# Differential attention in an encoder block: the weighted sum of a tile moved one step later on TensorE

## The chip, the cores and the metric

The kernel runs on one core of one Trainium2 chip. The metric is the device time of one execution in microseconds. The engines are called PE (TensorE: matrix products and transposes; PEld is its weight load), DVE (VectorE), ACT (ScalarE), POOL (GpSimd) and SP (SyncE, which issues DMAs). Each engine runs its own list of instructions in order, and the lists are tied together by semaphores alone: every wait and every count is written by hand.

## The reference, cut to what matters

One encoder layer over a prompt of 1024 tokens and a sample of 512, each with 16 learned meta tokens in front: a norm, one projection, eight heads of neighbourhood attention and four heads of differential attention, an output projection, and a mixture of 16 experts. The change lies in the differential heads:

```python
def _diff_attention(q, k, v, lam, lambda_init, subln):
    def attend(qb):
        s = jnp.einsum('bqhcd,bkhcd->bhcqk', qb, k).astype(jnp.float32) * scale
        p = jax.nn.softmax(s, axis=-1)
        a = (p[:, :, 0] - lam * p[:, :, 1]).astype(v.dtype)
        return jnp.einsum('bhqk,bkhe->bqhe', a, v)
...
    o = _rmsnorm(o, subln, SUBLN_EPS) * (1.0 - lambda_init)
```

Each head has two score maps (c = 0 and 1), each with its own softmax; their weighted difference multiplies the values.

## The kernel before, in words

A unit is one differential head; there are four, and the last (unit 3, `last` in the code) is treated apart. A unit has DS = 14 tiles of queries: two tails of 32 rows (meta tokens), then four tiles of the sample (512 keys each) and eight of the prompt (1024 keys each); in unit 3 the prompt's tiles come first. The loop over s goes through all of them as a software pipeline on PE, DVE and ACT, and in units 0 to 2 the projection for the next unit's queries, keys and values (`project`, 12 chunks, each in two halves of 12 products) is woven into the steps 0 to 11. Steps 12 to 14 have no projection.

What a tile n passes through:
- `scores` (L1706, PE): two products by key block, one for each map c, into PSUM banks 0 to 3.
- Evacuation of scores (L1285, DVE): out of PSUM into `e_df`, with the row's minimum for the softmax (`nmax`), for c = 0 and then 1.
- `scores_exp` (L889, ACT): the exponentials, with the sums (`ssum`).
- Combine (L1255 to L1260, DVE): the two maps become one.
- Turning (L1749 and L1751, PE): transposes of the combined weights into banks 4, 5 and, for the meta tokens, 6.
- `weights_to_rows` (L746 by way of `copy`, ACT) for bank 4, and copies by DVE (L1296, L1298) for banks 5 and 6, into `et_df`.
- Weighted sum (L1767 and L1769, PE): `et_df` times the values `v`, into bank 6 in units 0 to 2 and bank 7 in unit 3.
- `mix` (L1273, DVE): the sum, scaled, out of PSUM; SP stores it (L687).
- Squares of it (L880, ACT) for the norm.

The values of the next unit are turned by `v_rows` (L1586, L1588, PE) in steps 9 to 12, into bank 5, and copied out by `evac_v` (L1102, L1104, DVE). In units 0 and 1 (and once more in unit 0) `split_wq` splits the weights of a coming projection into a high part on ACT and a low part on DVE (L1091), in steps 5, 9 and 13. `rotate` (DVE) applies the rotary embedding to the next unit's queries and keys in steps 2 to 9; before it SP's `swap_halves` (L608) exchanges halves, once the rotation of the chunk before is done. In unit 3 `split_wo` does the same split for the output projection's weights.

At a unit's start PE makes products of 16 columns, the scores against the meta tokens (L1719, 52 of them); DVE turns these into `nsm` and `nmm`, for which `scores(0)` waits (`df_msn`).

The order on each engine in step s of units 0 to 2, before the change:
- PE: scores of s; projection half 0; turning of s-1; projection half 1; weighted sum of s-1; `v_rows`.
- DVE: `evac_v`; combine of s-1; `mix` of s-2; evacuation of scores of s; copies of s-1; splits; `rotate`.
- ACT: evacuation of the projection; splits; squares of s-3; copy of s-1; exponentials of s.

In unit 3 PE does scores of s, turning of s-1 and the weighted sum of s-2; DVE does combine of s-1, `mix` of s-3, evacuation of s, copies of s-1; ACT has the exponentials ahead of its copy. There the weighted sum of n waits for `mix` of n-1, since bank 7 is single:

```python
                        if last:
                            pe.wait_ge(df_mix, u * DS + n + CREDIT)
```

In units 0 to 2 it is turning that waits for `mix`, as the meta tokens' transpose shares bank 6 with the sum.

Of the kernel before, what the change touches and what calls it, by code (L numbers as in the profile page):

```python
# [26 lines left out]
ALU = mybir.AluOpType  # L27
# [3 lines left out]
P = 128  # L31
# [15 lines left out]
UNITS = 4  # L47
# [87 lines left out]
def build(nc, x_all, w_in, w_out, w_router, w_gate, w_up, w_down, rpb, meta_bias, lambdas, vecs,  # L135
# [12 lines left out]
    with ctx:  # L148
# [593 lines left out]
        def _(act):  # L742
# [120 lines left out]
            for u in range(UNITS):  # L863
                last = u == UNITS - 1
                for s in range(DS + 3 + last):
# [16 lines left out]
                    def scores_exp():  # L882
# [9 lines left out]

                    def weights_to_rows():
# [12 lines left out]
                    if not last and s < DS:  # L906
                        scores_exp()
# [131 lines left out]
        def _(dve):  # L1039
# [191 lines left out]
            for u in range(UNITS):  # L1231
# [14 lines left out]
                for s in range(DS + 3 + last):  # L1246
                    if not last and 0 <= s - 10 < 4:
                        evac_v(UNITS + u + 1, s - 10)
                    if 0 <= s - 1 < DS:
# [12 lines left out]
                                                 op0=ALU.mult, op1=ALU.add).then_inc(df_c, 1)  # L1262
                    n = s - 2 - last
# [12 lines left out]
                    if s < DS:  # L1276
                        t, rows, keep, k0, kt = DFS[u][s]
                        w = kt * P + N_META
                        if s >= 2:
                            dve.wait_ge(df_e, 2 * (u * DS + s - 1))  # L1280
                        dve.tensor_copy(e_df[0:rows, s % 2, :, kt * P:w], nsm[0:rows, :, t * N_META:(t + 1) * N_META])
                        for c in range(2):
                            dve.wait_ge(df_s, 2 * (u * DS + s) + c + 1)

                            dve.tensor_scalar(e_df[0:rows, s % 2, c, 0:kt * P],  # L1285
                                              ps[0:rows, 2 * c * BANK:2 * c * BANK + kt * P], -1.0,
                                              nmm[0:rows, c, t:t + 1], ALU.mult, ALU.min,
                                              accum_out=nmax[0:rows, s % 2, c:c + 1]).then_inc(df_m, 1)
# [258 lines left out]
        def _(pe):  # L1547
# [143 lines left out]
            for u in range(UNITS):  # L1691
# [17 lines left out]

                pe.wait_ge(qk_rot, ROPES * (u + 1))  # L1710
# [13 lines left out]
                v = vs[u % 2]  # L1724
# [6 lines left out]
                for s in range(1, DS + 1 + last):  # L1731
                    if s < DS:
                        scores(s)
                    if not last and s < NCH:
                        project(UNITS + u + 1, s, 0, 7, 1)
                    if s - 1 < DS:
                        n = s - 1
                        t, rows, keep, k0, kt = DFS[u][n]
                        b = n % 2
                        pe.wait_ge(v_evac, 4 * (u + UNITS + 1) + (0 if last else min(max(s - 9, 0), 4)) + CREDIT)  # L1740
                        pe.wait_ge(df_c, u * DS + n + 1)
                        pe.wait_ge(df_et_a, u * DS + n)
                        pe.wait_ge(df_et_d, u * DS + n + CREDIT)
                        if not last or n == 0:
                            pe.wait_ge(df_mix, u * DS + n + CREDIT)
                        if rows < P:
                            apart(pe)
                        for j in range(kt):
                            pe.transpose(ps[:, 4 * BANK + j * P:4 * BANK + j * P + rows],  # L1749
                                         e_df[0:rows, b, 0, j * P:(j + 1) * P], ident[0:rows, 0:rows])  # L1750
                        pe.transpose(ps[0:N_META, 6 * BANK:6 * BANK + rows],  # L1751
                                     e_df[0:rows, b, 0, kt * P:kt * P + N_META], ident[0:rows, 0:rows]).then_inc(df_t, 1)
                    if not last and s < NCH:
                        project(UNITS + u + 1, s, 1, 7, 1)
                    n = s - 1 - last
                    if 0 <= n < DS:
                        t, rows, keep, k0, kt = DFS[u][n]
                        b = n % 2
                        pe.wait_ge(df_et_a, u * DS + n + 1)
                        pe.wait_ge(df_et_d, u * DS + n + 1 + CREDIT)  # L1760
                        if last:
                            pe.wait_ge(df_mix, u * DS + n + CREDIT)
                        if rows < P:
                            apart(pe)
                        bank = 6 + last
                        o = ps[0:rows, bank * BANK + OCOL:bank * BANK + OCOL + P]
# [303 lines left out]
```

## Time and profile before

| | us |
|---|---|
| median of 3 runs | 3156.03 |
| lowest and highest run | 3152.79, 3158.81 |
| profiled execution, its own time | 3157.51 |
| span of the profiled execution, first to last instruction | 3155.7 |
| PE busy | 2971.7 (94%) |
| DVE busy | 1874.3 (59%) |
| ACT busy | 1478.7 (47%) |
| POOL busy | 174.9 (6%) |

The profiled execution lies 1.5 us above the median; the instructions span 1.8 us less than its time. Busy times of engines overlap, so they don't add up to the span. The four differential units run from 502.3 us (first 16-column products of unit 0) to about 999 us; before them lie the norm, the first projection and the neighbourhood heads, after them the output projection, the routing and the experts.

### The profile page before, as it was taken

The numbers are of one execution on the slowest core, as the hardware profiler recorded it, in microseconds if no ns is written. First come the engines' busy times: TensorE is split into PE (matmuls) and PEld (weight loads), VectorE is DVE, ScalarE is ACT, GpSimd is POOL, SyncE is SP. The second block draws the span as 40 slices with busy tenths as digits, with TensorE's granted clock in tenths as the row PEclk, the third lists the DMA queues.
The fourth block names the chain that finished last, engine by engine and source line by source line (L and its number), as shares of the span: only waits on it lengthen the run. The fifth ranks groups of instructions, "written<-read, shape, count | busy, mean of one in ns | idle before, by whom it ended". The sixth has DMA issues, their size and how long they took to land.

```text
span 3155.7 us, 49922 instructions
## 1 busy us (share of the span) xinstructions
PE 2971.7 (94%) x19549; PEld 2785.3 (88%) x19549; DVE 1874.3 (59%) x2998; ACT 1478.7 (47%) x2506; POOL 174.9 (6%) x179
## 2 busy tenths in 40 slices
PE   7999999999988993999999999999999999999993
PEld 6888888777855883999999999999999999999992
DVE  6223335755666346766766766766766666676672
ACT  4223322433334222655655655655555555565562
POOL 1000000000001000010011011010011011001001
PEclk9999999999989995999999999999999999999996
DMA  5322221110011434777877877778777777777774
GB/s 153 99 73 67 70 64 37 32 29 26 26 61 57 134 127 134 221 236 228 245 226 228 247 221 234 240 224 237 235 228 237 231 231 236 228 231 237 226 223 177
DMA packets 637872, 528.25 MB, mean 167 GB/s; under 512 B 30757, under 2 KB 618663, under 8 KB 637651
## 3 DMA queue, kind: packets, MB, share of 16 engines
q1 hardware_dynamic: 629458, 499.46, 51.1%
q0 software_dynamic: 8192, 25.70, 4.1%
q8 instruction: 156, 2.56, 0.3%
q14 instruction: 66, 0.53, 0.1%
HBM read 472.36 MB, written 40.79 MB: 163 GB/s over the span
## 4 chain that ended last, share of the span: by engine, by line
PE 75%; DVE 5%; DMA 2%; issue 1%; ACT 1%; POOL 0%; SPq 0%; DVEq 0%; POOLq 0%; ACTq 0%
PE ps L1889 39%; PE ps L1890 18%; PE ps L1574 5%; PE ps L1799 4%; PE ps L1769 2%; PE ps L1706 2%; DVE e_df L1285 1%; PE ps L1934 1%; PE ps L1749 1%; PE ps L1821 1%; PE ps L1883 1%; DMA y_dram<-yo 1%; PE ps L1767 1%; PE ps L1719 0%; DVE top_v L1370 0%
## 5 line engine op out<-in xcount | busy, mean ns | idle before, releaser
L1889 PE MATMUL ps<-xe,w_hi 128*128 128x392 f32 x4096 | 1195.6, 364 | 1.6 <-DVE xe L1480 1.6
L1890 PE MATMUL ps<-xe,w_lo 128*128 128x196 f32 x4096 | 1034.2, 252 | 0.0
L1467 DVE TENSOR_TENSOR w_lo<-raw,w_hi 128x2048 fp32r<-128x2048 f32 x384 | 875.5, 2284 | 0.2 <-issue 0.2
L1890 PEld LDWEIGHTS ps<-xe,w_lo 128*128 128x128 f32 x4096 | 784.1, 191 | 0.0
L1889 PEld LDWEIGHTS ps<-xe,w_hi 128*128 128x128 f32 x4096 | 770.2, 188 | 1.9 <-DVE xe L1480 1.9
L746 ACT ACTIVATE w_hi<-raw 128x2048 fp32r<-128x2048 f32 x384 | 731.8, 1910 | 11.8 <-DMA raw<-w_down_dram 11.8
L1889 PE MATMUL ps<-hid,w_hi 128*128 128x392 f32 x2048 | 609.4, 366 | 0.0
L1890 PE MATMUL ps<-hid,w_lo 128*128 128x196 f32 x2048 | 516.8, 252 | 0.0
L1890 PEld LDWEIGHTS ps<-hid,w_lo 128*128 128x128 f32 x2048 | 391.4, 191 | 0.0
L1889 PEld LDWEIGHTS ps<-hid,w_hi 128*128 128x128 f32 x2048 | 384.5, 188 | 0.0
L1500 DVE TENSOR_TENSOR gusum<-ps,part 128x392 f32<-128x392 f32 x256 | 145.0, 566 | 395.7 <-ACT part L746 395.7
L746 ACT ACTIVATE part<-ps 128x392 f32<-128x392 f32 x256 | 127.4, 498 | 511.5 <-PE ps L1890 511.5
L1574 PE MATMUL ps<-hT_hi,wq_hi 128*128 128x384 f32 (+1 forms) x768 | 284.8, 371 | 4.9 <-DVE hT_lo L1084 4.1
L1574 PE MATMUL ps<-hT_lo,wq_hi 128*128 128x384 f32 (+1 forms) x768 | 266.0, 346 | 0.0
L1574 PE MATMUL ps<-hT_hi,wq_lo 128*128 128x384 f32 (+1 forms) x768 | 265.7, 346 | 0.0
L1574 PEld LDWEIGHTS ps<-hT_hi,wq_hi 128*128 128x128 f32 x768 | 148.2, 193 | 36.9 <-issue 27.8
L1521 DVE TENSOR_TENSOR yT<-ps,y_part 128x196 f32<-128x196 f32 x128 | 46.2, 361 | 198.2 <-ACT y_part L746 196.4
L746 ACT ACTIVATE y_part<-ps 128x196 f32<-128x196 f32 x128 | 42.3, 330 | 249.2 <-PE ps L1890 249.2
L1574 PEld LDWEIGHTS ps<-hT_lo,wq_hi 128*128 128x128 f32 x768 | 148.6, 193 | 0.3
L1574 PEld LDWEIGHTS ps<-hT_hi,wq_lo 128*128 128x128 f32 x768 | 147.9, 193 | 0.4
L889 ACT ACTIVATE e_df<-e_df,nmax 128x1040 f32<-128x1040 f32 (+3 forms) x112 | 111.7, 1000 | 66.4 <-DVE e_df L1285 66.4
L2005 POOL DMA_INDIRECT residual_rows<-ye,idx_scatter x32 | 49.5, 1546 | 1619.8 <-DVE ye L1488 1614.9
(182 smaller groups left out, 3223.2 us busy)
## 6 DMA issues: line engine op xcount, KB each, us to landing
raw<-w_gate_dram SPq DMA_DIRECT2D x128, 1024.0 KB, 5.2
raw<-w_up_dram SPq DMA_DIRECT2D x128, 1024.0 KB, 5.2
raw<-w_down_dram SPq DMA_DIRECT2D x128, 1024.0 KB, 5.3
wqkv<-w_in_dram SPq DMA_DIRECT2D x24, 512.0 KB, 4.0
xt<-x_all_dram SPq DMA_DIRECT2D x12, 512.0 KB, 4.7
v_na<-v SPq DMA_DIRECT2D x64, 96.0 KB, 2.3
mixed_heads<-mix SPq DMA_DIRECT2D x96, 64.0 KB
mixs<-mixed_heads SPq DMA_DIRECT2D x12, 512.0 KB, 4.0
```

The lines of the kernel that those rows point to most:

```text
L746: return act.activation(out, in_, ACT.Copy, scale=scale)
L889: act.activation(e_df[0:rows, s % 2, c, 0:w], e_df[0:rows, s % 2, c, 0:w], ACT.Exp, bias=nmax[0:rows, s % 2, c:c + 1], scale=-1.0, accum_o ...
L1467: dve.tensor_tensor(w_lo[:, n % NW, :], raw[:, n % NRAW, :], w_hi[:, n % NW, :].bitcast(f32), ALU.subtract).then_inc(lo_done, 1)
L1500: dve.tensor_tensor(gusum[:, m % 2, :, :], src[:, :, 0:SLOTS], part[:, m % 2, :, :], ALU.add).then_inc(sum_done, 1)
L1521: dve.tensor_tensor(yT[:, d, :], ps[:, off:off + SLOTS], y_part[:, d % 2, :], ALU.add).then_inc(yT_done, 1)
L1574: ins = pe.matmul(ps[:, off:off + c1 - c0], wt[:, p, k, :], x[:, k, c0:c1], start=(k == 0 and j == 0), stop=(k == KD - 1 and j == 2))
L1706: ins = pe.matmul(ps[0:rows, o + j * 512:o + (j + 1) * 512], q, kT[f, (k0 + 4 * j) * P:(k0 + 4 * j + 4) * P], start=True, stop=True)
L1769: ins = pe.matmul(o, et_df[:, b, j * P:j * P + rows], v[:, k0 + j, :], start=False, stop=(j == kt - 1))
L1799: ins = pe.matmul(ps[0:rows, off:off + 512], x[:, b, k, 0:rows], w[:, k, n * 512:(n + 1) * 512], start=(k == 0 and j == 0), stop=(k == KD ...
L1889: pe.matmul(out, w_hi[:, slot, cols], x.rearrange("p h n -> p (h n)"), start=first, stop=False)
L1890: return pe.matmul(out[:, 0:SLOTS], w_lo[:, slot, cols], x[:, 0, :], start=False, stop=last)
L2005: pool.indirect_dma_start(out=acc_d, out_offset=bass.IndirectOffsetOnAxis(ap=idx_scatter[:, hh:hh + 1], axis=0), in_=ye[:, hh, :], in_offs ...
```

## The change: what it does

On PE, in units 0 to 2, the weighted sum of tile s-2 now stands in step s, between the scores of s and the projection half; `v_rows` follows it; then come the projection half, the turning of s-1 and the other half. The weighted sum of a unit's last tile moves into the next unit, behind its 16-column products. Turning waits for `mix` only ahead of its last transpose. On DVE the evacuation of scores comes ahead of `mix`, and `evac_v` behind it; this block of DVE's loop has no case apart for unit 3. On ACT the exponentials come ahead of the copy in all units, as they did in unit 3. PE's order in unit 3 stays.

```diff
@@ ACT
-                    if last and s < DS:
-                        scores_exp()
-                    if 0 <= s - 1 < DS:
-                        weights_to_rows()
-                    if not last and s < DS:
-                        scores_exp()
...
@@ DVE
                 for s in range(DS + 3 + last):
-                    if not last and 0 <= s - 10 < 4:
-                        evac_v(UNITS + u + 1, s - 10)
                     if 0 <= s - 1 < DS:
                         n = s - 1
...
+                    if s < DS:
+                        t, rows, keep, k0, kt = DFS[u][s]
+                        w = kt * P + N_META
+                        if s >= 2:
+                            dve.wait_ge(df_e, 2 * (u * DS + s - 1))
+                        dve.tensor_copy(e_df[0:rows, s % 2, :, kt * P:w], nsm[0:rows, :, t * N_META:(t + 1) * N_META])
+                        for c in range(2):
+                            dve.wait_ge(df_s, 2 * (u * DS + s) + c + 1)
+
+                            dve.tensor_scalar(e_df[0:rows, s % 2, c, 0:kt * P],
...
                     n = s - 2 - last
                     if 0 <= n < DS:
...
+                    if not last and 0 <= s - 9 < 4:
+                        evac_v(UNITS + u + 1, s - 9)
                     if 0 <= s - 1 < DS:
...
@@ PE
+                def turned_weights(n):
+                    t, rows, keep, k0, kt = DFS[u][n]
+                    b = n % 2
+                    s = n + 1
+                    pe.wait_ge(v_evac, 4 * (u + UNITS + 1) + (0 if last else min(max(s - 8, 0), 4)) + CREDIT)
+                    pe.wait_ge(df_c, u * DS + n + 1)
+                    pe.wait_ge(df_et_a, u * DS + n)
+                    pe.wait_ge(df_et_d, u * DS + n + CREDIT)
+                    if last and n == 0:
+                        pe.wait_ge(df_mix, u * DS + CREDIT)
...
+                    for j in range(kt):
+                        pe.transpose(ps[:, 4 * BANK + j * P:4 * BANK + j * P + rows],
+                                     e_df[0:rows, b, 0, j * P:(j + 1) * P], ident[0:rows, 0:rows])
+                    if not last:
+                        pe.wait_ge(df_mix, u * DS + n + CREDIT)
+                    pe.transpose(ps[0:N_META, 6 * BANK:6 * BANK + rows],
+                                 e_df[0:rows, b, 0, kt * P:kt * P + N_META], ident[0:rows, 0:rows]).then_inc(df_t, 1)
+
+                def weighted_values(uu, n):
+                    t, rows, keep, k0, kt = DFS[uu][n]
+                    b = n % 2
+                    v = vs[uu % 2]
+                    pe.wait_ge(df_et_a, uu * DS + n + 1)
+                    pe.wait_ge(df_et_d, uu * DS + n + 1 + CREDIT)
+                    if uu == UNITS - 1:
+                        pe.wait_ge(df_mix, uu * DS + n + CREDIT)
...
+                if u > 0:
+                    weighted_values(u - 1, DS - 1)
                 if not last:
                     project(UNITS + u + 1, 0, 0, 7, 1)
                 pe.wait_ge(df_msn, u + 1)
                 scores(0)
                 if not last:
                     project(UNITS + u + 1, 0, 1, 7, 1)
...
+                    for s in range(1, DS + 1):
+                        if s < DS:
+                            scores(s)
+                        if s >= 2:
+                            weighted_values(u, s - 2)
+                        if 0 <= s - 9 < 4:
+                            v_rows(UNITS + u + 1, s - 9)
+                        if s < NCH:
+                            project(UNITS + u + 1, s, 0, 7, 1)
+                        turned_weights(s - 1)
+                        if s < NCH:
+                            project(UNITS + u + 1, s, 1, 7, 1)
+                else:
+                    for s in range(1, DS + 2):
+                        if s < DS:
+                            scores(s)
+                        if s - 1 < DS:
+                            turned_weights(s - 1)
+                        if s >= 2:
+                            weighted_values(u, s - 2)
```

## Rows read from the trace of the kernel before

**Rows 1.** Busy time by stretch, unit 0: us, PE, PEld, DVE, ACT, POOL; clock, DMA

```profile
502.00:640.60 138.60, 130.33 (x765) 105.10 (x763) 85.45 (x200) 48.77 (x116) 0.00 (x0) 0.93 0.11 30
```

**Rows 2.** What PE waited for, 502 to 915 us: total us, times, longest

```profile
PE ps L1767 <- DVE et_df L1298: 15.8, 9, 2.1
PE ps L1749 <- DVE mix L1273: 6.6, 9, 1.0
PE ps L1767 <- ACT et_df L746: 1.5, 2, 0.8
```

**Rows 3.** Timeline, end of unit 0: start us, us, engine, line; in brackets idle before

```profile
610.38 0.35 PE L1574 MATMUL ps<-hT_lo,wq_hi 128*128 128x416 f32 x1
610.57 0.35 PE L1574 MATMUL ps<-hT_hi,wq_lo 128*128 128x416 f32 x1
610.85 0.48 PE L1767 MATMUL ps<-v,et_df 16*128 16x128 f32 x2
...
613.15 0.49 PE L1586 MATMUL ps<-ident,vT 128*128 128x128 f32 x3
...
615.88 0.34 DVE L1273 TENSOR_SCALAR mix<-ps,rec 128x128 f32<-128x128 f32 x1
...
616.37 1.07 PE L1749 MATMUL ps<-ident,e_df 128*128 128x128 f32 x8 [0.80 <-DVE mix L1273]
...
618.63 0.68 DVE L1296 COPY et_df<-ps 128x512 f32<-128x512 f32 x1
...
619.65 0.67 PE L1767 MATMUL ps<-v,et_df 16*128 16x128 f32 x2 [2.10 <-DVE et_df L1298]
...
640.63 3.02 PE L1719 MATMUL ps<-kT,qT 64*128 64x16 f32 x52
...
647.43 1.05 PE L1706 MATMUL ps<-kT,qT 64*32 64x512 f32 x4
```

**Rows 4.** Busy time by stretch, columns as in rows 1; the clock stands third last

```profile
620.00:622.00 2.00, 2.00 (x10) 1.78 (x10) 0.00 (x0) 1.79 (x6) 0.00 (x0) 0.50 0.00 0
...
644.00:646.00 2.00, 2.00 (x8) 2.00 (x8) 1.27 (x7) 0.00 (x0) 0.00 (x0) 0.50 0.00 0
```

**Rows 5.** Timeline, scores of a prompt tile in unit 0 and their evacuation

```profile
573.40 1.99 PE L1706 MATMUL ps<-kT,qT 64*128 64x512 f32 x8
...
575.42 1.28 DVE L1285 TENSOR_SCALAR_CACHE_REDUCE e_df<-ps,nmm 128x1024 f32<-128x1024 f32 x1 [1.47 <-PE ps L1706]
```

**Rows 6.** Timeline, unit 3: evacuations of steps 3 and 13, step 7 between

```profile
932.43 1.27 DVE L1285 TENSOR_SCALAR_CACHE_REDUCE e_df<-ps,nmm 128x1024 f32<-128x1024 f32 x1
...
957.06 1.28 DVE L1285 TENSOR_SCALAR_CACHE_REDUCE e_df<-ps,nmm 128x1024 f32<-128x1024 f32 x1
...
958.01 0.48 PE L1767 MATMUL ps<-v,et_df 16*128 16x128 f32 x2
...
958.44 1.16 ACT L889 ACTIVATE e_df<-e_df,nmax 128x1040 f32<-128x1040 f32 x1 [2.27 <-DVE e_df L1285]
...
959.47 0.69 DVE L1296 COPY et_df<-ps 128x512 f32<-128x512 f32 x1
...
960.40 1.99 PE L1706 MATMUL ps<-kT,qT 64*128 64x512 f32 x8
...
961.40 0.15 DVE L1255 RECIPROCAL rec<-ssum 128x2 f32<-128x2 f32 x1
...
963.29 1.06 PE L1749 MATMUL ps<-ident,e_df 128*128 128x128 f32 x8 [0.90 <-issue]
...
989.43 0.74 DVE L1285 TENSOR_SCALAR_CACHE_REDUCE e_df<-ps,nmm 128x512 f32<-128x512 f32 x1
```

**Rows 7.** PE's timeline, end of unit 2 and start of unit 3

```profile
882.58 0.48 PE L1767 MATMUL ps<-v,et_df 16*128 16x128 f32 x2
...
914.51 2.04 PE L1706 MATMUL ps<-kT,qT 64*32 64x512 f32 x4 [0.90 <-DVEq L1239]
...
922.29 4.88 PE L1706 MATMUL ps<-kT,qT 64*128 64x512 f32 x8
```

More of the change, by code:

```diff
@@ L881, in _ @@
                                        accum_out=ms_d[0:keep, t, u:u + 1]).then_inc(df_sq, 1)
-                    def scores_exp():
+                    if s < DS:
                         t, rows, keep, k0, kt = DFS[u][s]
@@ L891, in scores_exp @@
                                            accum_out=ssum[0:rows, s % 4, c:c + 1]).then_inc(df_e, 1)
-                    def weights_to_rows():
+                    if 0 <= s - 1 < DS:
                         n = s - 1
@@ L1262, in _ @@
                                                  op0=ALU.mult, op1=ALU.add).then_inc(df_c, 1)
+                    if s < DS:
[7 more added lines that the diff above has]
+                            dve.tensor_scalar(e_df[0:rows, s % 2, c, 0:kt * P],
+                                              ps[0:rows, 2 * c * BANK:2 * c * BANK + kt * P], -1.0,
+                                              nmm[0:rows, c, t:t + 1], ALU.mult, ALU.min,
+                                              accum_out=nmax[0:rows, s % 2, c:c + 1]).then_inc(df_m, 1)
                     n = s - 2 - last
@@ L1275, in _ @@
                                           rec[0:keep, n % 4, 0:1], None, ALU.mult).then_inc(df_mix, 1)
[L1276 to L1288, printed above, removed]
+                    if not last and 0 <= s - 9 < 4:
+                        evac_v(UNITS + u + 1, s - 9)
                     if 0 <= s - 1 < DS:
@@ L1708, in scores @@
                         ins.then_inc(df_s, 1)
+                def turned_weights(n):
[8 more added lines that the diff above has]
+                        pe.wait_ge(df_mix, u * DS + CREDIT)
+                    if rows < P:
+                        apart(pe)
+                    for j in range(kt):
[13 more added lines that the diff above has]
+                        pe.wait_ge(df_mix, uu * DS + n + CREDIT)
+                    if rows < P:
+                        apart(pe)
+                    bank = 6 + (uu == UNITS - 1)
+                    o = ps[0:rows, bank * BANK + OCOL:bank * BANK + OCOL + P]
+                    pe.matmul(o, et_df[0:N_META, b, 8 * P:8 * P + rows], v[0:N_META, FULL, :], start=True, stop=False)
+                    for j in range(kt):
+                        ins = pe.matmul(o, et_df[:, b, j * P:j * P + rows], v[:, k0 + j, :], start=False,
+                                        stop=(j == kt - 1))
+                    ins.then_inc(df_o, 1)
                 pe.wait_ge(qk_rot, ROPES * (u + 1))
@@ L1723, in _ @@
                     pe.wait_ge(na_mix, NS * UNITS + CREDIT)
-                v = vs[u % 2]
+                if u > 0:
+                    weighted_values(u - 1, DS - 1)
                 if not last:
@@ L1730, in _ @@
                     project(UNITS + u + 1, 0, 1, 7, 1)
[L1731 to L1766, printed above, removed]
-                        pe.matmul(o, et_df[0:N_META, b, 8 * P:8 * P + rows], v[0:N_META, FULL, :], start=True, stop=False)
-                        for j in range(kt):
-                            ins = pe.matmul(o, et_df[:, b, j * P:j * P + rows], v[:, k0 + j, :], start=False,
-                                            stop=(j == kt - 1))
-                        ins.then_inc(df_o, 1)
-                    if not last and 0 <= s - 9 < 4:
-                        v_rows(UNITS + u + 1, s - 9)
@@ new lines, in _ @@
+                    for s in range(1, DS + 1):
[12 more added lines that the diff above has]
+                    for s in range(1, DS + 2):
+                        if s < DS:
+                            scores(s)
[3 more added lines that the diff above has]
+                            weighted_values(u, s - 2)
```

## The prediction, made before the change was run

> **What bounds the kernel now.** I read the busy time by unit first. The differential part is four units; in unit 0, from 502 to 640.6 us, PE is busy 130.3 of 138.6 us and DVE 85.5 [rows 1]. Units 0 to 2, which the change names, are set by PE. Then the list of what PE waited for: up to the start of unit 3 the largest entry is the weighted sum (L1767) waiting for DVE's copy of the turned weights, 15.8 us in 9 waits; then turning (L1749) waiting for `mix`, 6.6 in 9; ACT's part of the copy costs 1.5 in 2 [rows 2]. The timeline shows where the nines sit: in the last three steps of each unit, where no projection half is left to stand between turning and weighted sum. In step 12 of unit 0 turning waits 0.80 for `mix` and the weighted sum 2.10 for the copy [rows 3]. Right behind, the granted clock is 0.50, the lower level of 1.2 GHz, and it is 0.50 again under the projection half that opens the next unit, behind 3.0 us of 16-column products [rows 3, 4].
>
> From the start of the weighted sum of step 11 to the first scores of the next unit, unit 0 takes 647.43 - 610.85 = 36.6 us; I take unit 1 as the same. Unit 2, whose next unit has no projection, takes 914.51 - 882.58 = 31.9 [rows 3, 7].
>
> Unit 3 has no projection; there I read one step on three engines: DVE goes from evacuation to copies to combine, PE waits 0.90 before turning [rows 6]. It is set by DVE.
>
> **The end of a unit, walked in the new order.** No instruction is added or removed, so the queues are walked with today's durations. Scores take 2.0 on PE, their evacuation on DVE starts 2.02 after them [rows 5] and lasts 2.4; ACT's first exponential starts 1.38 after the evacuation's start, both take, at 1.16 each, 2.4 with the reading; combine to turning 1.89; weighted sum 2.39; turning 1.1 [rows 6]. From `mix` to the PE that waits for it 0.49, from the copies to the weighted sum 1.02, three transposes of values are busy 0.49 [rows 3], overlapped 0.43 as an estimate, four 0.53. What follows PE starts, as an estimate, 0.1 behind it. Time zero is the start of the scores of step 12.
> - Step 12: scores to 2.0, weighted sum of tile 10 to 4.4, value rows to 4.9. DVE evacuates from 2.0 to 4.4, does `mix`, copies the value rows (an estimate of 0.9); turning needs that copy (they share a bank): 5.9. PE idle 1.0.
> - Step 13: turning to 7.0, scores to 9.0, weighted sum to 11.4, its copies long there (8.0). DVE: copies to 8.0, combine to 9.7, evacuation to 12.1, and only then `mix`. Turning runs from 11.4; its last transpose needs that `mix`, 12.6. Idle 0.2.
> - Step 14: ACT has the exponentials, 11.1 to 13.5, ahead of its copy, so the weighted sum starts at 14.2 (idle 1.5) and ends at 16.6. DVE splits weights in units 0 and 1 (an estimate of 1.2), so turning starts at 16.8 (idle 0.2), to 17.9. In unit 2 there is no split and no wait: 17.7.
> - Next unit: 16-column products to 20.9, the weighted sum of the last tile behind them to 23.3, projection half, 12 products of 0.19 [rows 3] less a tenth for narrower ones, 2.1, to 25.4. Into unit 3: `mix` and `nsm` now wait for that weighted sum, about 1.2 of PE idle where 0.90 was [rows 7]: 24.3.
>
> Full-clock gain: 36.6 - 25.4 = 11.2 twice, 31.9 - 24.3 = 7.6: 30.0. The value rows of step 11 now lie ahead of this stretch: 3 x 0.43 = 1.3 back.
>
> **Clock.** The projection half behind the 16-column products takes 3.8 us (647.43 less 640.63 and 3.02 [rows 3]) where 2.1 would do; the new order keeps those products, so 2 x 1.7 = 3.4 stay. Idle in an end becomes 2.9 us instead of 7.5 (a third of 15.8 and 6.6 [rows 2]), but transposes and waits still make stretches of 2.8 us without a product. The nearest row is the 0.50 after 0.80 and 2.10; I take one slow stretch of 1.7 a unit, 5.1, between none (0) and two (10.2).
>
> **Inside a unit.** The twelve steps with projection are PE's own work; the sum is moved, not shortened. Its copy now gets the scores as well as a projection half as cover. DVE's `mix` comes behind the evacuation, some 5.5 us into a step, PE's last transpose near 7.4 (scores, sum, half, turning): covered; without that cover its price is the 0.80 of [rows 3]. `evac_v` stands behind the same evacuation and is covered by the projection half. SP's stores follow `mix`, but stand behind `swap_halves`, which waits for a rotation later in the step, so nothing is late there; POOL takes no part. ACT's wait for its split of weights, which made the 1.5 [rows 2], could go; yet the exponentials stand behind that split now, and the copy behind them: I take 1.5 lost, between 1.5 won and 3 lost.
>
> A change of kind costs PE a little: the weighted sum at 610.85 starts 0.28 behind the last projection product, whose spacing is 0.19, so 0.09 [rows 3]. The new order trades projection to sum and sum to scores for projection to scores and scores to sum; no row has scores to sum. I take 0.03 a step for 39 steps, 1.2, between -3.5 and 3.5 (0.09 each).
>
> The Trainium skill (TensorE: Matmul & The Clock Gate, Part 2, step 1) says that PE pulls weight loads ahead of running products when rows don't conflict or they go to the background buffer. The trace does not agree at this place: the row at 610.85 names no wait, and the 0.09 is there. By the rule a sum that is ready a step earlier would hide its load, 3.5 us won instead of 1.2 lost, 3142.
>
> Units 0 to 2: 30.0 - 1.3 - 3.4 - 5.1 - 1.5 - 1.2 = 17.5 won; taking the bounds together, not all at once, 9 to 24.
>
> **Unit 3 is moved too.** DVE's block serves all units, so in unit 3 too `mix` of tile s-3 goes behind the evacuation of tile s. There PE's weighted sum of s-2 waits for that `mix` (one bank), and the next scores stand behind the sum. Today `mix` runs ahead of the evacuation, and the sum at 958.01 has it. From the evacuation of step 3 to that of step 13 unit 3 takes 989.43 - 932.43 = 57.0 us [rows 6]. In the new order there is a loop: evacuation 2.41, `mix` to PE 0.49, weighted sum 2.39, scores to the next evacuation 2.02: 7.3 a step, where today's mean is 5.7. Five steps have 7.3, and one with 32 rows in the sum, as an estimate, 7.1. In the last four the tiles are half as wide; with halves, as estimates, of evacuation (1.34), sum (1.5) and scores (1.16), they take 6.5, 5.4, 5.4 and 4.5. Together 65.5: 8.5 lost, between 7 and 10 by the estimates. It is zero only if PE did not need `mix`.
>
> **Sum.** 17.5 - 8.5 = 9.0 us won. The profiled execution took 3157.5 us (span 3155.7 and 1.8 around it), 1.5 above the median of 3156.0; the difference is taken off the median: 3147. Own range of this case 3140 to 3155. A measurement of this kernel can tell about 0.2%, 6.3 us, from no change.
>
> **Rivals.**
> - A: unit 3 does not lengthen, because its weighted sum gets `mix` in time. For it: PE has 0.90 to spare before turning in each step [rows 6]. Against: the wait is written, and `mix` comes 2.4 us later. Then 3156 - 17.5 = 3138.5.
> - B, slower: in unit 3 the new wait leaves PE idle 1.7 us (7.3 less 2.0, 1.1 and 2.4, rounded) in each step, and the granted clock falls to 0.50 there. At that clock scores took 4.88 at the start of unit 3 [rows 7], 2.9 more, and a sum, at half the clock, would take up to 2.4 more: 5.3 a step. Against: 0.90 in each step left the clock up. From 9.0 won to 6.3 lost are 15.3 us: it decides from three such steps on. With two it is 3158, with four 3168.
> - C: the ends of units keep their price: the granted clock stays at 0.50 through most of the new end, and the smaller waits add up with it. Gain 9, less 8.5: 3155.5.
> - The rule on weight loads: 3142, within the first case's range.
>
> **How the numbers follow.** Forecast 0.55, the weight-load rule 0.05, A 0.12, B 0.16, C 0.12. The likeliest gives 3147. Range 3138 to 3158: it leaves out the lower half of A (0.06) and most of B (0.12). Faster by over 0.2%: 0.43 of the forecast, the rule and A, 0.60. Slower: half of B, 0.08. Within: 0.32.
>
> **What would show it.** Ends of units 0 to 2: the waits of 2.10 for the copy gone, in their place 1.0 before turning in step 12, 0.2 for `mix`, 1.5 for ACT's copy; from the scores of step 12 to the next unit's first scores 25 to 31 us. Unit 3: PE waiting for `mix` ahead of the weighted sum, DVE for scores ahead of the evacuation, 65 us from the evacuation of step 3 to that of 13, and a granted clock near 1 in between (else B). It goes wrong if the slow clock comes back in the ends, or if unit 3's loop has slack that I don't see.

## The result, and the profile after

| | before | changed |
|---|---|---|
| median of 5 runs each, us | 3156.32 | 3139.63 |
| lowest and highest run | 3152.79, 3158.81 | 3137.03, 3141.70 |
| span of the profiled execution | 3155.7 | 3137.8 |

The ratio is 0.9941, with a 95% interval of 0.9929 to 0.9953: 16.7 us or 0.6% faster. The forecast was 3147, 9 us won. The time lies inside the range of 3138 to 3158, but the gain is nearly twice the forecast one. A second set of five runs (run c1_changed_again) gave 3141.90, a ratio of 0.9953 [0.9939, 0.9966] to the kernel before beside it; its profile is called the second profile below. One execution of a later run (old steps, new ends) took 3840.7 us at a granted clock of 0.68, and that run's median and ratio leave it out.

The page of the changed kernel:

```profile
span 3137.8 us, 49916 instructions
...
PE 2959.9 (94%) x19549; PEld 2777.0 (89%) x19549; DVE 1872.9 (60%) x2998; ACT 1483.5 (47%) x2506; POOL 173.0 (6%) x179
```

PE has the same 19549 products, and its busy time is 11.8 us less. The busy time by stretch in unit 0, which answers to [rows 1], and below it the stretches that answer to [rows 4] (the clock stands third last):

```profile
499.20:627.20 128.00, 125.08 (x746) 100.44 (x745) 83.86 (x198) 49.25 (x113) 0.00 (x0) 0.94 0.12 32
...
622.00:624.00 2.00, 1.76 (x11) 1.64 (x12) 1.93 (x5) 0.48 (x3) 0.00 (x0) 0.86 0.03 8
624.00:626.00 2.00, 2.00 (x12) 2.00 (x11) 1.06 (x2) 0.00 (x0) 0.00 (x0) 0.50 0.00 0
632.00:634.00 2.00, 2.00 (x11) 2.00 (x11) 0.00 (x0) 0.00 (x0) 0.00 (x0) 0.50 0.00 0
634.00:636.00 2.00, 2.00 (x9) 2.00 (x8) 1.12 (x4) 0.41 (x2) 0.00 (x0) 0.50 0.02 5
```

What PE waited for in units 0 to 2 (total, times, longest), which answers to [rows 2]:

```profile
PE ps L1734 <- ACT et_df L746: 4.6, 5, 1.2
PE ps L1715 <- DVE v L1096: 2.5, 3, 0.8
...
PE ps L1719 <- DVE mix L1276: 1.1, 5, 0.3
```

The nine waits for DVE's copy (15.8 us) are gone, and of the 6.6 for `mix` 1.1 is left; in their place stand the three that the walk named, 8.2 in sum. PE's timeline of the end of unit 0, from the scores of step 12 to the first scores of unit 1, which answers to [rows 3]:

```profile
608.42 1.99 PE L1698 MATMUL ps<-kT,qT 64*128 64x512 f32 x8
610.35 0.48 PE L1734 MATMUL ps<-v,et_df 16*128 16x128 f32 x2
...
612.65 0.49 PE L1578 MATMUL ps<-ident,vT 128*128 128x128 f32 x3
...
614.09 1.09 PE L1715 MATMUL ps<-ident,e_df 128*128 128x128 f32 x8 [0.84 <-DVE v L1096]
...
620.74 0.28 PE L1719 MATMUL ps<-ident,e_df 128*16 128x128 f32 x1 [0.25 <-DVE mix L1276]
622.24 0.48 PE L1734 MATMUL ps<-v,et_df 16*128 16x128 f32 x2 [1.23 <-ACT et_df L746]
622.65 3.10 PE L1736 MATMUL ps<-v,et_df 128*128 128x128 f32 x16
...
627.26 3.02 PE L1749 MATMUL ps<-kT,qT 64*128 64x16 f32 x52
...
630.92 3.78 PE L1736 MATMUL ps<-v,et_df 128*128 128x128 f32 x16
634.35 0.67 PE L1566 MATMUL ps<-hT_hi,wq_hi 128*128 128x384 f32 x1
...
637.88 1.05 PE L1698 MATMUL ps<-kT,qT 64*32 64x512 f32 x4
```

The end takes 637.88 - 608.42 = 29.5 us where the old one took 36.6. The idle times 0.84, 0.25 and 1.23 stand where the walk put 1.0, 0.2 and 1.5. At the lower clock are the weighted sum at 622.65 (3.10 us against 2.05), the one behind the 16-column products (3.78), and the projection half from 634.35, 3.5 us long.

Unit 3, on PE and DVE, which answers to [rows 6, 7], with the clock of one stretch:

```profile
887.71 1.17 PE L1698 MATMUL ps<-kT,qT 64*32 64x512 f32 x4 [1.14 <-DVEq L1231]
...
904.53 1.28 DVE L1262 TENSOR_SCALAR_CACHE_REDUCE e_df<-ps,nmm 128x1024 f32<-128x1024 f32 x1
...
929.20 0.45 PE L1734 MATMUL ps<-v,et_df 16*128 16x128 f32 x2 [1.80 <-DVE mix L1276]
...
932.36 2.81 PE L1698 MATMUL ps<-kT,qT 64*128 64x512 f32 x8
...
935.20 1.28 DVE L1262 TENSOR_SCALAR_CACHE_REDUCE e_df<-ps,nmm 128x1024 f32<-128x1024 f32 x1 [2.42 <-PE ps L1698]
...
938.11 0.45 PE L1734 MATMUL ps<-v,et_df 16*128 16x128 f32 x2 [1.80 <-DVE mix L1276]
...
972.80 0.75 DVE L1262 TENSOR_SCALAR_CACHE_REDUCE e_df<-ps,nmm 128x512 f32<-128x512 f32 x1 [0.18 <-PE ps L1698]
...
932.00:936.00 4.00, 4.00 (x19) 2.09 (x18) 1.57 (x3) 0.00 (x0) 0.00 (x0) 0.74 0.00 0
```

The forecast's loop is there: PE waits 1.80 for `mix` ahead of the weighted sum, and DVE for the scores behind it. From the evacuation of step 3 to that of step 13 it takes 972.80 - 904.53 = 68.3 us, where the kernel before had 57.0 [rows 6] and the forecast 65.5. One step (929.20 to 938.11) takes 8.9 us instead of 7.3: its scores took 2.81 us instead of 1.99, in a stretch with a mean granted clock of 0.74.

**Where the 17.9 us between the two spans lie.** Ahead of the first scores of unit 0 (511.31 before, 508.87 after) 2.4; from there to the first scores of unit 3 24.4 (403.2 to 378.8); in unit 3, to the first transposes behind it, -10.2 (84.9 to 95.0); behind it 1.3. The stage that was changed won 14.2. In the second profile of the changed kernel (span 3137.7) the same four are 1.6, 26.6, -9.9 and -0.3, so there the stage won 16.7. Over the eleven profiles of this study the first scores of unit 0 lie between 506.7 and 513.7 us, and what follows unit 3 takes 2154.7 to 2157.5 us, though the code of neither part differs: the first and the last of the four terms lie within that spread.

### The profile page after: what moved, and what is told of

Read it like the earlier page. It is cut to its first block, busy times and chain, and to the rows that moved or that the text cites. A ratio compares the mean times of both kernels' runs of the same rounds, so it can differ in the third digit from the quotient of the medians.

```text
span 3137.8 us, 49916 instructions
## 1 busy us (share of the span) xinstructions
PE 2959.9 (94%) x19549; PEld 2777.0 (89%) x19549; DVE 1872.9 (60%) x2998; ACT 1483.5 (47%) x2506; POOL 173.0 (6%) x179
## 4 chain that ended last, share of the span: by engine, by line
PE 76%; DVE 4%; DMA 2%; issue 1%; ACT 1%; POOL 0%; SPq 0%; DVEq 0%; POOLq 0%; ACTq 0%
PE ps L1897 39%; PE ps L1898 18%; PE ps L1566 5%; PE ps L1807 4%; PE ps L1736 3%; PE ps L1698 3%; PE ps L1942 1%; PE ps L1715 1%; DVE e_df L1262 1%; PE ps L1829 1%; PE ps L1891 1%; DMA y_dram<-yo 1%; PE ps L1734 1%; PE ps L1749 0%; DVE top_v L1362 0%
## 5 line engine op out<-in xcount | busy, mean ns | idle before, releaser
L1566 PEld LDWEIGHTS ps<-hT_hi,wq_hi 128*128 128x128 f32 x768 | 147.9, 193 | 16.1 <-issue 7.0
```

The source lines that it names most:

```text
L1566: ins = pe.matmul(ps[:, off:off + c1 - c0], wt[:, p, k, :], x[:, k, c0:c1], start=(k == 0 and j == 0), stop=(k == KD - 1 and j == 2))
```

## The experiments

**Unit 3: undo the order there, or make only that change.** In both, `mix` moves on DVE in unit 3 alone; in the first against the changed kernel, in the second against the kernel before. The edit shown is that of the first; in the second the two conditions change places.

```diff
+                    if last:
+                        mix_rows()
 ...                  # evacuation of scores
-                    mix_rows()
+                    if not last:
+                        mix_rows()
```

> The changed kernel with one thing undone: in unit 3 alone, VectorE does mix ahead of the evacuation again. Theory: the loop evacuation, mix, weighted sum, scores is what lengthened unit 3, and nothing else there is lost. Then from the evacuation of step 3 to that of step 13 it takes 57 us again (68.3 in the changed kernel), TensorE's waits for mix ahead of the weighted sum vanish, and the time is 3139.6 - 11.3 = 3128. Rival: 8.5 us of the loss is the loop, as forecast, and the other 2.8 is something that stays without it (the clock, or another order of queues): then about 60 us and 3131. Rival A, that unit 3 loses nothing by the order: 3139 to 3140.

> The kernel before with one thing done: in unit 3 alone, VectorE does mix behind the evacuation. Theory: the loop needs only this order, so unit 3's stretch of ten steps goes from 57 to 68 us and the time from 3156 to 3167; units 0 to 2 keep their ends of 36.6, 36.6 and 31.9. Rival: the loss as forecast by the loop alone, 8.5, gives 3164.5; if the clock stays up in this kernel and falls only in the changed one, the steps are 7.3 throughout and the lower number comes out. If unit 3 lengthens only together with the other parts of the change (ACT's order is the same in unit 3): 3156.

Measured: 3131.26, ratio 0.9917 [0.9905, 0.9930], and 3166.60, ratio 1.0031 [1.0020, 1.0043]. In the first, the evacuations of steps 3 and 13 and the stretch whose clock stood at 0.74:

```profile
904.99 1.27 DVE L1279 TENSOR_SCALAR_CACHE_REDUCE e_df<-ps,nmm 128x1024 f32<-128x1024 f32 x1
...
962.00 0.74 DVE L1279 TENSOR_SCALAR_CACHE_REDUCE e_df<-ps,nmm 128x512 f32<-128x512 f32 x1
...
932.00:936.00 4.00, 3.10 (x20) 1.72 (x19) 3.93 (x10) 3.13 (x8) 0.00 (x0) 1.00 0.00 0
```

57.0 us again, at full clock: the loop and the slow stretches go together. The unit itself is 11.2 shorter than in the changed kernel (95.0 to 83.9), the median 8.4. By stage the rest is 2.0 won in units 0 to 2 and 2.4 lost both ahead of them and behind unit 3, where the code is the same. The second run lengthens unit 3 by 10.8 with no other part of the change. Its stretch takes 66.9, with one slow step; so does that of the second profile of the changed kernel, where the first has two slow places and 68.3. Rival A and the thought that the other parts are needed both fall.

**Steps up to 11 in the old order, first try.** Only PE's order is put back, ACT and DVE stay as changed:

```diff
-                        if s >= 2:
+                        if s >= NCH:
                             weighted_values(u, s - 2)
 ...
+                        if s < NCH - 1:
+                            weighted_values(u, s - 1)
```

> The changed kernel with the weighted sum of steps up to 11 back in its old place, behind the second projection half of its own step; from step 12 on the new order. Theory: in the steps with projection the new place itself saves time, because the sum is followed by projection products and not by scores: a prompt step takes 9.72 again where the changed kernel has 9.53, so about 5 to 7 us slower than the changed kernel, 3145 to 3147. Forecast's term (a change of kind costs 0.03 a step more in the new place): about 1 us faster than the changed kernel, 3138.5. Third: the place makes no difference, and the 5.5 us lie in the waits for ACT's copy: 3139.6, with steps of 9.5.

Measured: 3161.59, ratio 1.0011 [1.0003, 1.0020], 22 us slower than the changed kernel; none of the three expectations holds. The waits of PE in units 0 to 2:

```profile
PE ps L1734 <- ACT et_df L746: 8.6, 7, 2.2
PE ps L1715 <- DVE v L1094: 6.0, 9, 0.7
```

Prompt steps do take 9.72 again, but the version made waits of its own: turning waits 6.0 for the copy of the value rows, which the sum no longer covers, and ACT's copy, now behind the exponentials, is late for the sum (8.6 against 4.6). It shows that the parts of the change need each other and leaves their sizes open.

**Steps up to 11 in the old order on all three engines**, the ends and unit 3 as changed:

```diff
 # PE
-                        if s >= 2:
+                        if s >= NCH:
                             weighted_values(u, s - 2)
 ...
+                        if s < NCH - 1:
+                            weighted_values(u, s - 1)
+                        if 0 <= s - 9 < 2:
+                            v_rows(UNITS + u + 1, s - 9)
 ...
 # DVE
+                    if not last and s < NCH:
+                        mix_rows()           # ahead of the evacuation
 # ACT
+                    if not last and s < NCH:
+                        scores_exp()         # behind the copy
```

> The changed kernel with the steps up to 11 of units 0 to 2 as before on all three engines (weighted sum of s-1 at the end of its step, mix ahead of the evacuation, ACT's copy ahead of the exponentials, value rows of steps 9 and 10 at the end); the ends from step 12 on and unit 3 stay as changed. The value rows of step 11 stay behind the scores, and the wait of turning for their copy, some 0.5 us a unit, is this version's own and is to be taken off. Theory from the traces: the steps with projection gained about 1 us a unit by the sum's new follower and nothing by ACT's waits, so this version is 3 to 4 us slower than the changed kernel, plus its own 1.5: 0.9967 of the kernel before, 3145 to 3147 where the changed kernel has 3140 to 3142. Forecast: the new place costs 1.2 and ACT's waits another 1.5, so this version would be 2.7 faster, less its own 1.5: 3139 to 3140.

Measured: 3149.09, ratio 0.9980 [0.9971, 0.9990]. From first scores to the scores of step 12 its units take 101.0, 101.1 and 100.2 us; the second profile of the changed kernel has 98.7, 98.6 and 97.6: 7.5 less. Its own wait was larger than expected:

```profile
PE ps L1729 <- DVE v L1100: 2.7, 3, 0.9
```

With 2.7 taken off, the new order of the steps is worth 4.8 us, a little more than the theory's 3 to 4 (3.8 against the first profile, which has a slow step at its start). (Step 12 also got longer, 7.16 for 6.79, by a wait of 1.20 for the value rows in place of 0.84.) The forecast, 2.7 in the other direction, is wrong.

**The weighted sum between the first projection half and turning**, in steps 2 to 11. Two things come with it: DVE copies the value rows of steps 9 to 11 ahead of `mix`, and their turning on PE waits for DVE's copies of the step before.

```diff
-                        if s >= 2:
+                        if s >= NCH:
                             weighted_values(u, s - 2)
+                            pe.wait_ge(df_et_d, u * DS + s - 1 + CREDIT)   # ahead of v_rows
 ...                      # value rows, projection half 0
+                        if 2 <= s < NCH:
+                            weighted_values(u, s - 2)
                         turned_weights(s - 1)
```

> The changed kernel with the weighted sum of steps 2 to 11 between the first projection half and turning: what follows the sum is now turning, neither scores nor projection; the value rows stay behind the scores. It asks what the 0.17 us hangs on that a prompt sum takes longer when scores follow (2.39, in the run with the old place 2.40) than when projection follows (2.22). Theory 1, the price belongs to the scores behind short products: a sum followed by turning takes 2.2, steps stay at 9.53, TensorE's two waits for ACT's copy in a unit (0.43 and 0.51) vanish behind the half that now covers them, and the time is within 2 us of the changed kernel. Theory 2, only projection hides its load behind the sum and every other follower pays: 2.39 before turning, 0.15 for 30 sums or so, 4 to 5 us slower than the changed kernel, 3144. Against both: the copy of step s-2 and the turning of s-1 now meet in one place, and a wait of turning for mix of about 0.3 in each step would add up to 9 us, 3148.

Measured: 3148.77, ratio 0.9974 [0.9965, 0.9984]; the changed kernel beside it had 3141.90. A sum and what follows it, first in this version, then in the kernel before, then in the changed kernel (where two answers follow each other):

```profile
571.08 0.48 PE L1736 MATMUL ps<-v,et_df 16*128 16x128 f32 x2
...
573.38 1.04 PE L1717 MATMUL ps<-ident,e_df 128*128 128x128 f32 x8
```

```profile
580.73 0.48 PE L1767 MATMUL ps<-v,et_df 16*128 16x128 f32 x2
...
583.12 0.31 PEld L1706 LDWEIGHTS ps<-kT,qT 64*128 64x128 f32 x4
583.12 1.14 PE L1706 MATMUL ps<-kT,qT 64*128 64x512 f32 x4
```

```profile
570.68 0.48 PE L1734 MATMUL ps<-v,et_df 16*128 16x128 f32 x2
...
572.90 0.42 PE L1566 MATMUL ps<-hT_hi,wq_hi 128*128 128x384 f32 x1
...
580.20 0.29 PEld L1734 LDWEIGHTS ps<-v,et_df 16*128 16x128 f32 x2 [0.76 <-issue]
580.20 0.48 PE L1734 MATMUL ps<-v,et_df 16*128 16x128 f32 x2
...
580.62 1.86 PEld L1736 LDWEIGHTS ps<-v,et_df 128*128 128x128 f32 x16
580.62 2.05 PE L1736 MATMUL ps<-v,et_df 128*128 128x128 f32 x16
...
582.39 0.36 PEld L1578 LDWEIGHTS ps<-ident,vT 128*128 128x128 f32 x3
582.50 0.49 PE L1578 MATMUL ps<-ident,vT 128*128 128x128 f32 x3
```

From the sum's start to the next kind it takes 2.30 with turning behind it, 2.39 with scores, 2.22 with projection. A meeting is a block on PE together with the block behind it. These are the meetings of prompt steps (the tiles with 1024 keys) at full clock, from these timelines; the time is from the block's start to the start of the next:

| block | followed by | us |
|---|---|---|
| weighted sum, prompt | projection; turning or value rows; scores | 2.22; 2.30; 2.39 |
| projection half, 384 columns | turning; sum or scores | 2.20 to 2.22; 2.28 to 2.31 |
| three value rows | projection; scores | 0.25; 0.42 |
| scores, prompt | projection; sum | 1.92 to 1.93, either |

The step of the kernel before (scores, half, turning, half, sum) is 1.93 + 2.21 + 0.91 + 2.28 + 2.39 = 9.72; the changed one (scores, sum, half, turning, half) 1.93 + 2.22 + 2.20 + 0.90 + 2.28 = 9.53; this version's (scores, half, sum, turning, half) 1.92 + 2.31 + 2.30 + 0.91 + 2.29 = 9.73. So the place of the sum sets the step by what stands behind each block. Theory 2 holds in kind and not in size: the sum ahead of turning does lose, but 0.08 and not 0.17, and a second loss that it did not name, 0.1 a step, comes with it: the half ahead of the sum no longer has turning behind it. The wait for `mix` feared in each step did not come (0.7 us in all, in the ends), so that its 3148 is close to the measured time is chance.

**Old ends, new steps.**

```diff
-                        if s >= 2:
+                        if 2 <= s <= NCH:
                             weighted_values(u, s - 2)
 ...
+                        if s >= NCH:
+                            weighted_values(u, s - 1)
 ...                      # and no sum behind the next unit's 16-column products
 # DVE: mix ahead of the evacuation, ACT: copy ahead of the exponentials, for s >= NCH
```

> The changed kernel with the ends of units 0 to 2 as before: from step 12 on the weighted sum stands at the end of its own step, the last one in its own unit, VectorE does mix ahead of the evacuation and ACT its copy ahead of the exponentials; steps up to 11 and unit 3 stay as changed. Theory: the gain is made in the ends, 22 us by the two traces, so the time is 3139.6 + 22 = 3162, slower than the kernel before, because unit 3's loss stays; TensorE waits again about 2.1 for the copy in steps 12 to 14, and the ends take 36, 36 and 32 us from the sum of step 11's tile to the next scores. Forecast: its own terms for the ends (30.0 less 3.4 less 5.1, with the split wait 1.5) give 20 to 21.5, that is 3160. Rival: most of the gain lies in the steps with projection: below 3150.

Measured: 3167.96, ratio 1.0031 [1.0020, 1.0042]. From the scores of step 12 to the next first scores the ends take 36.8, 37.7 and 33.1 us, 24.6 more than the changed kernel's. What PE waited for in units 0 to 2:

```profile
PE ps L1746 <- DVE et_df L1302: 13.3, 9, 2.3
PE ps L1727 <- DVE v L1102: 9.5, 3, 3.2
```

The nine waits for the copy are back. The 9.5 for the value rows is this mixture's own (the kernel before has no such wait in its ends), so the 24.6 is not a clean price; that the gain is made in the ends is clear, that it is 22 rests on the two traces.

**ACT's part undone in units 0 to 2.**

```diff
-                    scores_exp()
-                    weights_to_rows()
+                    if last:
+                        scores_exp()
+                    weights_to_rows()
+                    if not last:
+                        scores_exp()
```

> The changed kernel with ACT's part undone in units 0 to 2: the copy of s-1 ahead of the exponentials of s. Forecast: ACT's new order costs 1.5 us by the split of weights and 1.5 idle in step 14 of each unit; so without it the wait of 1.2 ahead of the weighted sum of step 14 shrinks to about 0.5, but the exponentials of tile 13 come some 2 us later, and with them combine and the last turning, which waits about 1 us: between 1 us faster and 3 us slower than the changed kernel. Theory from the changed kernel's trace: the waits for the split are 1.3 us in all with the new order and 1.5 with the old one, so nothing is to be had in the steps with projection, and the end of a unit gets longer by 0.5 to 1: 3141 to 3143. Rival: a copy first makes the exponentials late in every step (9.5 us long), and combine, turning with them: more than 10 us slower.

Measured: 3149.27, ratio 0.9973 [0.9962, 0.9984], 7.4 slower than the changed kernel beside it, more than either theory. Steps 13 and 14 of unit 0 on PE:

```profile
625.31 1.06 PE L1721 MATMUL ps<-ident,e_df 128*128 128x128 f32 x8 [0.54 <-issue]
628.02 0.28 PE L1725 MATMUL ps<-ident,e_df 128*16 128x128 f32 x1 [1.65 <-DVE mix L1282]
629.36 0.76 PE L1740 MATMUL ps<-v,et_df 16*128 16x128 f32 x2 [1.06 <-DVE et_df L1296]
```

With the copy first, the exponentials of tile 12 come later, with them combine, DVE's evacuation of the scores behind it, and `mix` behind that: 1.65 where the changed kernel waits 0.25. In units 0 to 2 the waits for `mix`, value rows and issue grow from 1.1, 2.5 and 0.2 to 6.3, 3.6 and 2.3, those for the copies go from 4.6 (ACT) to 3.2 (DVE): 7.0 in all. The profiled execution is the slowest of its seven (3158.58), and its ends are 12.4 us longer than in the second profile; what is beyond the 7.0 stands mostly at the lower clock (0.50 from 630 to 634 us). The steps up to 12 take 99.6, 98.7 and 97.6, as in the changed kernel: the rival of late exponentials in every step falls too.

**Two waits taken away:** the order in unit 3 as in the first run, and in step 12 the value rows ahead of the sum, their copy ahead of `mix`. Only PE's part is shown.

```diff
+                        if s == NCH:
+                            pe.wait_ge(df_et_d, u * DS + s - 1 + CREDIT)
+                            v_rows(UNITS + u + 1, 3)
                         if s >= 2:
                             weighted_values(u, s - 2)
-                        if 0 <= s - 9 < 4:
+                        if 0 <= s - 9 < 3:
                             v_rows(UNITS + u + 1, s - 9)
```

> The changed kernel with the two waits taken away that its trace shows as new: in unit 3 VectorE does mix ahead of the evacuation (as in the run where that was undone alone, 3131.3), and in step 12 of units 0 to 2 the value rows stand ahead of the weighted sum on TensorE, their copy ahead of mix on VectorE, so that the sum covers the copy. Theory: the wait of 0.84 before turning in step 12 vanishes, three times, 2.5 us, and with it some of the slow clock behind it: 3127 to 3129. Rival: the wait only moves, as mix, now 0.8 later, holds up the last transpose of step 13 (0.25 now, 1.0 then): 3131.

Measured: 3126.40, ratio 0.9908 [0.9895, 0.9922], the best version here, 31 us below the kernel before on the same chip; its interval overlaps that of the run with unit 3 alone undone. The end of unit 0, and the clock of a stretch:

```profile
613.54 1.09 PE L1723 MATMUL ps<-ident,e_df 128*128 128x128 f32 x8 [0.25 <-DVE v L1096]
...
626.71 3.02 PE L1757 MATMUL ps<-kT,qT 64*128 64x16 f32 x52
629.66 0.48 PE L1742 MATMUL ps<-v,et_df 16*128 16x128 f32 x2
630.07 2.05 PE L1744 MATMUL ps<-v,et_df 128*128 128x128 f32 x16
631.88 0.42 PE L1574 MATMUL ps<-hT_hi,wq_hi 128*128 128x384 f32 x1
...
634.18 1.05 PE L1706 MATMUL ps<-kT,qT 64*32 64x512 f32 x4
...
632.00:634.00 2.00, 2.00 (x14) 1.92 (x12) 1.66 (x8) 0.40 (x2) 0.00 (x0) 1.00 0.11 33
```

The wait fell from 0.84 to 0.25 and did not move to `mix` (0.25 as before), so the rival falls. Step 12 became 0.43 shorter, three times 1.3 us. The ends take 25.9, 24.7 and 25.4 us: the rest of their gain on the changed kernel is the clock, since behind the same 16-column products the weighted sum took 2.2 and the half 2.3 us in units 0 and 1. That the shorter wait did this is not shown: in unit 0 of the run with the old steps they took 2.22 and 2.28 too, behind a wait of 1.20. That end and unit 0 here had a slow weighted sum (3.93) ahead of those products instead; unit 1 here had none. Unit 2 gained nothing, and the first two steps of unit 3 take 16.1 us instead of 14.0 in the run with unit 3 alone undone.

**The changed kernel again.**

> The changed kernel once more, unaltered, so that the times of these runs can be set beside its own on the same chip: 3139.6, between 3137 and 3142. By stage: if the first 16-column products of unit 0 lie between 499 and 503.5 us from the start, the 3.0 us by which they came earlier in its first profile are spread of the part ahead of the change; if they lie at 499.3 again, where the kernel before has 502.3 and 503.1, the change did something ahead of unit 0.

Measured: 3141.90, ratio 0.9953 [0.9939, 0.9966]. The first 16-column products of unit 0 lie at 500.3, inside the 499 to 503.5 that the expectation took for spread, and in the other runs between 497.4 and 504.1. Its ends take 28.2, 28.2 and 25.4.

## Why the prediction was right in part and wrong in part: by its own steps

| step | forecast, us won | first profile | second profile |
|---|---|---|---|
| ends of units 0 to 2 (30.0 - 3.4 - 5.1) | 21.5 | 22.3 | 23.5 |
| steps with projection (-1.3 - 1.5 - 1.2) | -4.0 | 2.1 | 3.1 |
| unit 3 | -8.5 | -10.2 | -9.9 |
| stage | 9.0 | 14.2 | 16.7 |

**Right: the mechanism and the ends.** The ends were walked from durations of the trace, and waits and places came out as walked. At full clock they were to take 25.4, 25.4 and 24.3; they took 29.5, 28.2 and 25.3, an excess of 7.9, against 8.5 set aside for the clock. Set beside the same blocks at full clock (in the mended version the sum behind the 16-column products takes 2.22, the half behind it 2.29), the slow ones cost about 9.3 in the first profile and 8.1 in the second. Either leaves 73.7 for the three ends at full clock, where the walk had 75.1.

**Partly right: the slow half behind the 16-column products.** The forecast kept 3.4 us since those products stay. The half lost 1.2 and 0.7 in units 0 and 1 of the first profile (3.52 and 3.01 for 2.29), 1.2 and 0.8 in the second; the sum ahead of it, which the walk had at full clock, lost 1.9 in each, out of the 5.1 set aside for one more slow stretch a unit. In units 0 and 1 of the mended version, in unit 0 of the run with the old steps, in unit 1 of the first try and in unit 0 of the run with ACT's part undone they stay too, and the half takes 2.28 to 2.30, as at full clock. In the old order it did so once, 2.31 in unit 1 of the run that changes unit 3 alone, where the kernel before has 3.85 and 3.84. So the products alone do not set it, as the forecast had it; what does is open.

**Wrong: "a change of kind", 1.2 lost.** This is the step that failed: the price of the meetings inside a unit. The forecast priced the new meetings at 0.03 a step and wrote that no row showed scores to sum. The new meetings cost nothing more: scores take 1.92 ahead of the sum as ahead of projection, and the half takes 2.28 ahead of scores as ahead of the sum. What the old order paid, and the forecast left out, was the meeting that disappears: sum to scores, 2.39 against 2.22 ahead of projection and 2.30 ahead of value rows. Per unit the ten sums of these steps take 18.92 us before and 17.95 after, without waits: 2.9 us won in three units. Likewise the value rows: the forecast moved three groups at 0.43 into these steps, 1.3 lost; behind the sum and ahead of projection each takes 0.25, so three take 0.74 where two took 0.84: 0.3 won.

**Wrong: ACT's waits, 1.5 lost.** In the steps with projection PE waited 1.5 for ACT's copy before; after, 0.94 for it and 0.36 for `mix`: 0.2 won. The value taken was the worse half of a range whose other end was 1.5 won. Nor is ACT's order a cost in the ends: undone, it costs 7.4.

Together 2.9 + 0.3 + 0.2 = 3.4 won instead of 4.0 lost. The second profile shows 3.1; in the first, one slow step at the start of unit 0 (4.2 instead of 3.3) takes 0.9 of it. The run with the old steps gives 4.8, from the other side.

**Right as mechanism, a little small: unit 3.** Loop steps take 7.29, forecast 7.3; the forecast's 65.5 for ten steps plus two slow stretches (8.91 for 7.3, and 7.81 for 6.5) make the 68.3. That is rival B's mechanism, at 1.6 and 1.3 instead of 5.3 a time; the second profile has the 1.6 alone. The unit's start gives 1.1 back.

The measured 3139.6 is close to rival A's 3138.5, by another way: unit 3 did lengthen. Rival C falls with the ends. Of the 17.9 and 18.0 us between the spans, 3.7 in the first profile and 1.3 in the second lie outside the stage, within the spread named above.

**The weight-load rule.** The loads (PEld) in the rows above: the value rows' load, of 128 rows behind 128-row products, starts at 582.39, 0.11 ahead of its product. The scores' load, 64 rows high behind the sum's 128, starts at 583.12 with its own product; so does the load of the sum's 16 rows behind the 64-row scores (580.20), and so does the sum's first load of 128 rows behind the 16-row products (580.62). The Trainium skill (TensorE: Matmul & The Clock Gate, Part 2, step 1) says that PE pulls weight loads ahead of running products when rows don't conflict or the load goes to the background buffer. The trace agrees where a load is as high as the one ahead of it, and does not where the height changes, in either direction. That the change of height is the cause was not tried by itself.

By the table a change of height behind a projection half costs 0.08, and scores behind a sum 0.17 (2.39 for 2.22); behind scores it makes no difference whether the half or the sum follows. The old step has three such changes between its blocks (scores to half, half to sum, sum to scores), the new one two (scores to sum, half to scores). The rule's rival had the sign and nearly the size (3.5 won; 2.9 measured), and its reason holds for about half of it: the sum's own load still starts with its product, but behind scores that costs no more than the half's load did there, where it cost 0.08 behind the half. The other half is the scores' load, 0.17 behind a sum and 0.08 behind a half.

## What to carry to other kernels

When an instruction group is moved, price all its old and new meetings, the ones that disappear first: the trace of before had the same sum at 2.39 ahead of scores and 2.30 ahead of value rows. A block of a loop that serves several stages must be walked in each of them: here 10 of some 25 us went back through a unit that the change did not name, and one condition (`if last`) returned them in that unit. The cost of the lower clock was forecast well as a sum over several stretches (8.5; about 9.3 and 8.1 in the two profiles), and badly stretch by stretch.

## What the runs showed of the hardware that was not expected

- A weight load as high as the one ahead of it started 0.11 us ahead of its product (582.39 for 582.50); where the height changed, from 128 rows to 64 (583.12), from 64 to 16 (580.20) or from 16 to 128 (580.62), it started with it. A sum took 2.22, 2.30 or 2.39 us by what followed it.
- The same work stood at either clock level from run to run: the weighted sum behind the 16-column products of units 0 and 1 took 4.14 to 4.16 us in most runs of the new ends, 3.81 in two, and 2.22 or 2.23 in three (both units of the mended version, unit 0 of the run with the old steps). In two of these three the slow stretch lay ahead of those products (0.55 and 0.60 at 622 to 626 us in the mended version, 0.57 at 626 to 630 in the other), in the third there was none.
- In unit 3, where a step takes 7.29 us with 1.80 of idle time, the step from the evacuation of step 6 to that of step 7 took 8.91 to 8.93 in all eight profiles of that order (stretches at 0.74 to 0.83 in the first), a second slow one came in five of them, and the other full steps took 7.2 to 7.3. The steps of 6.4 with 0.90 had none in the three profiles of the other order.
